# Five state-space products laid whole into the prompt attention, four attention output products into the sample attention

## What is computed

```python
glu = zg * sigmoid(zg @ w_glu + b_glu)              # branch A, the state-space model, 512 wide
a_br = glu @ w_ssm_out                              # 576 x 512 by 512 x 1024
b_br = o_nsa @ w_nsa_out                            # branch B, sparse attention, 576 x 512 by 512 x 1024
merged = sigmoid(g_a) * a_br + sigmoid(g_b) * b_br
x = x + merged @ w_o
```

## Time and profile before

| | |
|---|---|
| median of 3 runs | 796.8 us (795.71 to 800.57) |
| span of the profiled execution | 795.5 us |
| PE, matmuls | 762.2 us busy, 96% |
| PE, weight loads | 494.9 us busy, 62% |
| DVE | 379.9 us busy, 48% |
| ACT | 204.9 us busy, 26% |
| POOL | 106.8 us busy, 13% |
| the chain that ended last | PE 80%, DMA 8%, DVE 6%, issue 2%, ACT 2%, POOL 1% |
| prompt attention | 294 to 405 us |
| sample attention | 405 to 450 us |
| products and merge | 450 to 486 us |

### The profile page before, as it was taken

The page is one execution under the profiler, slowest core; times in us unless marked ns, Lnnn a source line. Parts: engine busy times, 40 slices in busy tenths (PEclk is TensorE's granted clock), DMA queues, the critical chain, the costliest instruction groups (busy, mean ns, idle before and its releaser), DMA issues.

```text
span 795.5 us, 12983 instructions
## 1 busy us (share of the span) xinstructions
PE 762.2 (96%) x5070; PEld 494.9 (62%) x5070; DVE 379.9 (48%) x850; ACT 204.9 (26%) x485; POOL 106.8 (13%) x160
## 2 busy tenths in 40 slices
PE   8999999999999999889999999999999999998995
PEld 5455588777778788555566775445556564654442
DVE  3269523997232323766624378434732212214865
ACT  3011213112223354654523200134111111123223
POOL 3000006000000311334500100011111101015002
PEclk9999999999999999999999999999999999999998
DMA  9640493841440499200030279003799999996002
GB/s 324 160 126 0 112 278 139 99 133 57 140 97 17 139 233 266 94 1 1 1 120 2 96 216 384 1 14 128 282 407 409 416 418 416 417 373 211 17 14 106
DMA packets 81287, 136.50 MB, mean 172 GB/s; under 512 B 33926, under 2 KB 57546, under 8 KB 77010
## 3 DMA queue, kind: packets, MB, share of 16 engines
q1 hardware_dynamic: 64700, 110.17, 41.7%
q0 software_dynamic: 3728, 13.38, 4.9%
q10 hardware_dynamic: 12798, 12.12, 4.6%
HBM read 116.55 MB, written 21.19 MB: 173 GB/s over the span
## 4 chain that ended last, share of the span: by engine, by line
PE 80%; DMA 8%; DVE 6%; issue 2%; ACT 2%; POOL 1%; DVEq 0%; SPq 0%; POOLq 0%; ACTq 0%
PE ps L1215 29%; PE ps L1300 10%; PE ps L1656 6%; PE ps L1904 5%; PE ps L1788 4%; PE ps L1222 3%; PE ps L1776 3%; DMA merged<-in_w_exp_down 3%; DMA w_slot<-in_w_exp_down 2%; PE ps L1441 2%; PE ps L1820 2%; PE ps L1491 2%; PE ps L1537 2%; PE ps L1518 2%; DMA wgu<-expert_rows,pos_i 1%
## 5 line engine op out<-in xcount | busy, mean ns | idle before, releaser
L1215 PE MATMUL ps<-w_slot,hT 128*128 128x396 f32 (+1 forms) x192 | 71.1, 529 | 0.6 <-DMA w_slot<-in_w_in 0.4
L1215 PE MATMUL ps<-hT,w_slot 128*128 128x288 f32 x256 | 63.1, 407 | 0.0
L1215 PEld LDWEIGHTS ps<-hT,w_slot 128*128 128x128 f32 x256 | 48.3, 190 | 13.9 <-issue 0.8
L1215 PEld LDWEIGHTS ps<-w_slot,hT 128*128 128x128 f32 x192 | 36.1, 190 | 32.5 <-issue 13.4
L2987 DVE SCALAR_TENSOR_TENSOR th<-th,ps 128x256 f32<-128x256 f32 x12 | 5.1, 421 | 103.2 <-ACT th L2248 103.2
L1788 PE MATMUL ps<-w_slot,hT 128*32 128x256 f32 x544 | 49.7, 380 | 0.0
L1300 PE MATMUL ps<-hT,w_slot 128*128 128x288 f32 x144 | 37.3, 407 | 0.0
L1215 PE MATMUL ps<-qg,w_slot 128*128 128x288 f32 x128 | 33.7, 408 | 0.0
L1788 PEld LDWEIGHTS ps<-w_slot,hT 128*32 128x32 f32 x544 | 26.3, 110 | 10.0 <-issue 2.3
L2728 DVE TENSOR_REDUCE nm_p<-ps 128x2 f32<-128x256 f32 (+3 forms) x32 | 25.0, 819 | 15.6 <-PE ps L1491 15.5
L1300 PEld LDWEIGHTS ps<-hT,w_slot 128*128 128x128 f32 x144 | 27.3, 190 | 7.6 <-issue 0.2
(11 more groups left out here) (508 smaller groups left out, 1416.5 us busy)
## 6 DMA issues: line engine op xcount, KB each, us to landing
merged<-in_w_exp_down SPq DMA_DIRECT2D x10, 1024.0 KB, 15.9
w_slot<-in_w_in SPq DMA_DIRECT2D x8, 1024.0 KB, 7.7
wgu<-in_w_exp_gate SPq DMA_DIRECT2D x8, 1024.0 KB, 12.1
wgu<-in_w_exp_up SPq DMA_DIRECT2D x8, 1024.0 KB, 14.1
w_slot<-in_w_exp_gate SPq DMA_DIRECT2D x8, 1024.0 KB
w_slot<-in_w_exp_up SPq DMA_DIRECT2D x8, 1024.0 KB
w_slot<-in_w_exp_down SPq DMA_DIRECT2D x6, 1024.0 KB
expert_rows<-onsaT ACTq DMA_DIRECT2D x12, 512.0 KB, 8.2
```

Of the source, the lines that this page charges most:

```text
L1215: ins = pe.matmul(out, a, b, start=(n == 0), stop=(n == len(pairs) - 1))
```

## The change

Five of the sixteen state-space products (m, h) = (0, 0), (0, 1), (1, 0), (1, 1), (2, 0) leave the sample attention and are laid at five places of the prompt attention. Each is whole: eight matmuls of the trace in one piece, into bank 6 or 7, which are free between two blocks there. ACT copies each out at a place of the list chosen for it (`ab_out` steps), and the values of the next block wait for that copy. In the sample attention, the eleven that are left take the first eleven iterations, and the four attention output products (0, 0), (1, 0), (2, 0), (3, 0) the last four: they use prompt rows only. DVE takes these four in the place of ACT, multiplies by the gate, and writes the result over the gate. The merge behind then has two operations for these four halves instead of three. Twelve `bb` products are left for the tail. `ab_out` lies in other tiles (a new one for m = 0 and 1, the end of `kvct` for 2, the queries for 3, keys and values for 4 to 7). Pairs of semaphores with separate times are joined into one, and one tile is allocated later in the list; neither changes an order.

```diff
-    steps, late, jobs = [], [], list(range(len(AB_JOBS)))
+    steps, late = [], []
+    jobs = [("ab", j) for j in range(AB_EARLY, len(AB_JOBS))] + [("bb", j) for j in range(len(BB_EARLY))]
...
-        steps.append(("ab", jobs.pop(0)))
-    return steps + [("ab", j) for j in jobs]
+        steps.append(jobs.pop(0))
+    return steps + jobs
...
+AB_BEFORE = {("vcs", 0, 0): [("ab", 0, 0), ("ab", 0, 1)], ("t", 2, 0): [("ab_out", 0, 0)],
...
+AB_BANK = [6, 7, 6, 6, 7]
+AB_OF_BLOCK = [1, 2, 4, 5]
...
-PROMPT = prompt_steps()
+PROMPT = [new for step in prompt_steps() for new in AB_BEFORE.get(step, []) + [step]]
...
+                elif what == "ab":
+                    if i == 0 and c == 0:
+                        pe.wait_ge(glu_made, 8)
+                        pe.wait_ge(*w_need["so"])
+                        pe.wait_ge(cmp_taken, COMPRESSED["kc", 0])
+                    elif i == 1 and c == 0:
+                        pe.wait_ge(cmp_taken, COMPRESSED["vcs", 0])
+                    elif i == 2 and c == 0:
+                        pe.wait_ge(pr_taken, 1)
+                    elif i == 3 and c == 0:
+                        pe.wait_ge(ab_taken, 3)
+                    elif i == 4 and c == 0:
+                        pe.wait_ge(pr_taken, 2)
+                    m, h = AB_JOBS[i]
+                    for j in (2 * c, 2 * c + 1):
+                        ins = pe.matmul(ps[:, AB_BANK[i], 0:HALF], wk("so", D, 0, 4)[:, j, P * m:P * m + P],
+                                        gluT[:, j, HALF * h:HALF * h + HALF], start=(j == 0), stop=(j == 3))
+                    if c:
+                        ins.then_inc(ab_made, 1)
...
+                    if first:
+                        pe.wait_ge(ab_taken, AB_OF_BLOCK[b])
...
+                elif what == "ab_out":
+                    m, h = AB_JOBS[i]
+                    act.wait_ge(ab_made, i + 1)
+                    act.activation(ab_out[m][:, HALF * h:HALF * h + HALF], ps[:, AB_BANK[i], 0:HALF], ACT.Copy).then_inc(ab_taken, 1)
...
+                elif what == "bb":
+                    m, h = BB_EARLY[i]
+                    dve.wait_ge(tg_ld[m], 16)
+                    v = gates[:, m, 1, HALF * h:HALF * h + HALF]
+                    o = take(("bb", m, h))
+                    empty(dve.scalar_tensor_tensor(v, v, 1.0, o[:, 0:HALF], ALU.add, ALU.mult))
+
+            dve.wait_ge(pe_done, PLAN.done(("o", len(GROUPS) - 1)))
+            dve.wait_ge(ab_taken, AB_EARLY)
```

More of the change, by code:

```diff
@@ L129 @@
 AB_JOBS = [(m, h) for m in range(KD) for h in range(2)]
+AB_EARLY = 5
+BB_EARLY = [(m, 0) for m in range(4)]
 def attention_steps():
-    steps, late, jobs = [], [], list(range(len(AB_JOBS)))
+    steps, late = [], []
+    jobs = [("ab", j) for j in range(AB_EARLY, len(AB_JOBS))] + [("bb", j) for j in range(len(BB_EARLY))]
     n = len(ITEMS)
@@ L376, in make_plan @@
             p.add(("ab",) + AB_JOBS[i], "act")
+        elif what == "bb":
+            p.add(("bb",) + BB_EARLY[i], "dve")
     for m in range(KD):
         for h in range(2):
-            p.add(("bb", m, h), "dve")
+            if (m, h) not in BB_EARLY:
+                p.add(("bb", m, h), "dve")
     for what, t, c in second_norm_steps():
@@ L516, in build @@
             onsaT = sb("onsaT", [P, 4, ROWS], stack=late)
-            ab_out = [(flat(qT) if m < 4 else flat(kv))[:, ROWS * (m % 4):ROWS * (m % 4 + 1)] for m in range(KD)]
             with ExitStack() as at:
@@ L1546, in _, with merge_product @@
             pe.wait_ge(qs_made, 1)
+            def merge_product(m, h):
+                cut = slice(HALF * h, HALF * h + HALF)
+                o = begin(("bb", m, h))
+                finish(product(o[:, 0:HALF], [(wk("no", D, 0, 4)[:, j, P * m:P * m + P], onsaT[:, j, cut]) for j in range(4)]))
             for what, i in attention_steps():
+                if what == "bb":
+                    pe.wait_ge(*w_need["no"])
+                    merge_product(*BB_EARLY[i])
+                    continue
                 if what == "ab":
@@ L1614, in _ @@
             pe.wait_ge(*emptied(("o", len(GROUPS) - 1)))
-            pe.wait_ge(*w_need["no"])
             for m in range(KD):
                 for h in range(2):
-                    cut = slice(HALF * h, HALF * h + HALF)
-                    o = begin(("bb", m, h))
-                    finish(product(o[:, 0:HALF], [(wk("no", D, 0, 4)[:, j, P * m:P * m + P], onsaT[:, j, cut]) for j in range(4)]))
+                    if (m, h) not in BB_EARLY:
+                        merge_product(m, h)
             def last_rows_through_w_o():
@@ L2026, in _ @@
             act.activation(sm[:, 9], sm[:, 6], ACT.Sin)
-            act.activation(sm[:, 10], sm[:, 7], ACT.Sin).then_inc(trig, 1)
+            act.activation(sm[:, 10], sm[:, 7], ACT.Sin).then_inc(dt_trig, 1)
             for t in range(NT - 1):
@@ L2798, in _ @@
                     cut = slice(HALF * h, HALF * h + HALF)
-                    dve.wait_ge(*emptied(("ab", m, h)))
+                    if AB_JOBS.index((m, h)) >= AB_EARLY:
+                        dve.wait_ge(*emptied(("ab", m, h)))
                     link(dve.scalar_tensor_tensor(mt[:, 0], gates[:, m % 4, 0, cut], 1.0, ab_out[m][:, cut], ALU.add, ALU.mult))
-                    o = take(("bb", m, h))
-                    empty(dve.scalar_tensor_tensor(mt[:, 1], gates[:, m % 4, 1, cut], 1.0, o[:, 0:HALF], ALU.add, ALU.mult))
+                    if (m, h) in BB_EARLY:
+                        second = gates[:, m, 1, cut]
+                    else:
+                        o = take(("bb", m, h))
+                        second = mt[:, 1]
+                        empty(dve.scalar_tensor_tensor(second, gates[:, m % 4, 1, cut], 1.0, o[:, 0:HALF], ALU.add, ALU.mult))
                     dve.wait_ge(*emptied(("bb", m, h)))
-                    tt(merged[:, m, cut], mt[:, 0], mt[:, 1], ALU.add).then_inc(merged_made, 1)
+                    tt(merged[:, m, cut], mt[:, 0], second, ALU.add).then_inc(merged_made, 1)
                     dve.wait_ge(merged_made, 2 * m + h + 1)
```

28 lines of the change are left out of this document (15 added, 13 removed), and 4 rows, old and new, of the table AB_BEFORE.

## The result

The changed kernel takes **790.1 us** (median of 5 runs, 789.1 to 792.0), the kernel before 796.8 us (794.9 to 800.6, 5 runs). The ratio is 0.991, with a 95% interval of 0.988 to 0.994. The forecast was 790.9 us within 1% of before, and both hold. The profiled execution has a span of 788.2 us, against 795.5.

The account below looks back on a forecast made before the run. TensorE (PE), busy 96% of the span, was taken as the bound. Tail -9.70 plus prompt attention +3.86 gave -5.84 us: profiled 789.7, median 1.3 above the span, so 790.9 us, range 787.5 to 795.0.

Parts of the forecast that it names:

- tail and loop: Sample attention loop keeps its length with 15 products; the tail goes from 18 products to 13, giving 9.70 us.
- first place: Prompt attention, before the compressed sample values: the product partly fills PE's 1.29 us wait for DVE's copy, +0.65 us.
- second place: Prompt attention, before the transposes of unit 4: no idle time to fill, so the full +2.04 us.
- third place: Prompt attention, before the compressed turn of unit 6: the product fills 0.85 us idle for DVE's copy, +1.11 us.
- fourth and fifth: Prompt attention, two products around the compressed scores of block 2, laid into PE's waits there: +1.04 us for both.
- ACT's copy at the fifth: ACT takes the fifth product behind unit 11's first exponentials, ahead of a turned copy, so the bank frees late: +0.45 us.
- clock: Prompt attention at 361 to 362 us: granted clock, 0.50 before, expected to stay high with pauses filled, -1.43 us.
- prompt part: Net cost of five early products in the prompt attention: 5.29 - 1.43 = 3.86 us, bounds nothing to 10.2.
- That more would be hidden: Rival: prompt attention has room for all 10.2 us by weight-load busy time, 785.7 us; chance 0.15.
- That the low clock stays: Rival: the low clock stays in the prompt attention or shows at another pause, 792.3 us; chance 0.17.
- No bank held PE: Rival: PE stands at banks awaiting ACT's copies at the five prompt attention places, +9 us, 800; chance 0.06.
- no gate came late: Rival: in the merge, the first of four gate tiles takes 7 us instead of 4, 792.9 us; chance 0.08.

Follow-up runs that it names:

- the first experiment: Changed kernel with all sixteen attention output products back in the tail, none in the last four sample attention steps; 796.3 us.
- the two experiments with these pauses, filled and open: Filled: kernel before plus idle transposes in two pauses of block 2, 797.3 us. Open: changed kernel without its fourth and fifth early products, 795.1 us.
- without fourth and fifth: Changed kernel without the two early products around the compressed scores of block 2, two attention output products more in the tail; 795.1 us.
- prompt part alone: Changed kernel with the five early state-space products kept and the four attention output products back in the tail; 796.3 us.
- gates behind `w_o`: Changed kernel with the load of `wo1` put ahead of the last four gate tiles, so these land later; 796.3 us.
- the kernel with the clock alone: Kernel before with unused transposes, seven ahead of block 2's compressed scores and twelve ahead of unit 11's masks, no product moved; 797.3 us.

## Why the prediction was right, step by step

The same numbers as the prediction's, now from rows of the changed kernel; a cost is the change in the distance between two starts. This is PE's timeline of the changed kernel at the first place, the third, and around the compressed scores of block 2, against the earlier trace rows:

```profile
319.04 0.43 PE L1469 MATMUL ps<-hT,cx 128*32 128x128 f32 x8 [0.30 <-ACT cx L2200]
319.40 2.21 PE L1500 MATMUL ps<-qg,w_slot 128*128 128x288 f32 x8
...
343.38 1.09 PE L1555 MATMUL ps<-ident,hT 128*128 128x128 f32 x8
344.31 2.11 PE L1500 MATMUL ps<-qg,w_slot 128*128 128x288 f32 x8
346.25 0.27 PE L1550 MATMUL ps<-ident,pc 128*128 128x128 f32 x1
346.36 0.60 PE L1540 MATMUL ps<-ident,caches 128*128 128x128 f32 x4
...
357.08 1.09 PE L1555 MATMUL ps<-ident,work 128*128 128x128 f32 x8
358.01 2.11 PE L1500 MATMUL ps<-qg,w_slot 128*128 128x288 f32 x8
359.95 1.00 PE L1511 MATMUL ps<-kcbd,qg 128*128 128x64 f32 x8
360.79 2.16 PE L1500 MATMUL ps<-qg,w_slot 128*128 128x288 f32 x8
362.78 0.39 PE L1522 MATMUL ps<-causal,ident_b 128*128 128x128 bf16 x4
363.10 1.56 PE L1528 MATMUL ps<-kt,qg 64*128 64x384 f32 x8
...
366.63 1.39 PE L1555 MATMUL ps<-ident,hT 128*128 128x128 f32 x8
```

| step | predicted | measured | from |
|---|---|---|---|
| tail and loop | -9.70 | -9.70 | marks |
| first place | +0.65 | +0.78 | 319.04 to 321.54, was 1.72 |
| second place | +2.04 | +2.04 | rows above |
| third place | +1.11 | +0.68 | 343.38 to 346.36, was 340.91 to 343.21 (the cached keys' turns) |
| fourth and fifth | +1.04 | +0.74 | 357.08 to 363.10, was 353.98 to 359.26 |
| ACT's copy at the fifth | +0.45 | +0.29 | eight transposes, 366.63 to 367.94, less 1.02 of pitch |
| clock | -1.43 | -1.58 | 363.10 to 368.96 (next masks) less 0.29, was 359.26 to 366.41 |
| prompt part | +3.86 | +2.93 | marks |

- **The tail was exact.** 104 matmuls in 25.22 us, and the fifteen steps of the sample attention kept their length with attention output products in four of them. That those four were not free to leave out is what the first experiment shows: they stand in pauses that PE would have otherwise.
- **The prompt part was charged 0.93 us too much**, the one part of the sum with errors of size. The mis-sized term is the pitch. I had taken 2.04 us for a product and 1.02 for eight turns, from rows in other surroundings. At the third and fourth places a product takes 1.94 (344.31 to 346.25, 358.01 to 359.95) and the turns ahead of it 0.93. The fifth takes 1.99 (360.79 to 362.78), the second the full 2.04, and the first, ahead of the narrow compressed values, 2.14 (319.40 to 321.54). What sets the pitch I did not work out. At the third place a short pause ahead of the cached keys' turns is filled as well: from the turn before to these 0.35 us in the kernel before, 0.11 now. The third, fourth and fifth places and ACT's copy together give 0.89 back, the clock 0.15, and the first place takes 0.13.
- **The clock came back as forecast.** The scores of unit 11 take 1.56 us again, and the two experiments with these pauses, filled and open, show each direction, each in one traced execution. The extra 0.15 us lies in the values behind the turns, which ran at the low level too (1.17 us from 363.20 to the next start, 1.02 at full clock) and which I had left out.
- **The merge kept up.** The new wait of DVE stands where it was forecast, 2.73 us long instead of 3.6. SP reached the gates earlier than I had taken it to, 10.9 us behind the start of the tail (463.79 less 452.85) and not 11.9, and the first tile landed 4.2 us later. DVE's timeline:

```profile
468.06 0.46 DVE L2856 SCALAR_TENSOR_TENSOR mt<-hT,kv 128x288 f32<-128x288 f32 x1 [2.73 <-DMA hT<-gates_by_features]
...
479.33 0.46 DVE L2407 TENSOR_TENSOR merged<-mt 128x288 f32<-128x288 f32 x1
```

and the row of PE that needs all sixteen halves:

```profile
481.60 7.09 PE L1240 MATMUL ps<-w_slot,merged 128*64 128x512 f32 x32
```

  The last half is ready at 479.79, so the cover is 1.8 us where I had worked out 1.0. Moving the loads in both directions shows that it is real: less wait brings nothing, and 4.9 us more of it exposes 3.15, which gives a cover of 4.87 - 3.15 = 1.7 us.
- **The rivals.** That more would be hidden is out: the second place paid in full. That the low clock stays is out for this stretch. No bank held PE, and no gate came late. So the sum was the forecast's, and the 0.8 us between 790.9 and 790.1 is of the size of the over-charged terms; with a scatter of some microseconds between executions, I don't claim more. Two of the prediction's sums were off, and neither bears on the forecast: 796.8 - 5.84 is 791.0 and not 790.9, and with 3 us more at each of the five places the banks would have cost 15 us, +9 on the kernel before, which is 806 us and not 800.
- **Where the margin was thin.** Three parts lost more when undone than the pauses that this opens: 7.05 us where they are 3.61 (four products), 5.3 where 4.4 was expected (fourth and fifth), 5.8 where 3.15 is exposed (gates). The forecast survived since the change opens no new pause of PE, not since I had understood what an open one costs; to that extent it was luck.

## What to carry to other kernels

Find room for matmul work by the idle time in PE's timeline at the very place, not by a busy share of a stretch: of five equal products, four cost 0.5 to 0.8 us each and one its full 2.04. When a stage's work is moved about, count a pause of PE that is opened or closed with what the granted clock does behind it, and read the windows for a few microseconds after it. A wait that is hidden today has a cover that can be worked out from two rows; write it down, since the next change will spend it.

## What the runs showed of the hardware that I had not expected

In the four places of the table a pause of PE, or several close together, costs its own length and then 0.6 to 1.2 times that again, for the clock goes to its low level behind it and stays there for some microseconds while PE is busy. The price is the stretch's time less the same instructions' time at full clock:

| kernel | idle on PE | ended at | low clock after | its price |
|---|---|---|---|---|
| before | 0.99, 0.51, 1.08 with short work between | 359 us | to past 363 us | 1.6 us |
| without fourth and fifth | 0.72, 0.51, 1.09 | 362.4 | past 368 us | 2.7 us |
| prompt part alone | 0.94, 0.97, 1.08, 0.62 | 451.9 | to about 458 us | 3.1 us |
| gates behind `w_o` | 3.15 in one | 484.4 | to about 490 us | 2.9 us |

In the second kernel the scores of unit 11 start at 362.76 and the next masks at 371.05, 8.29 us, against 5.57 for the same in the kernel with the clock alone (359.45 to 365.02). The changed kernel still has 5.00 us of pauses in its prompt attention, one of 1.14 us among them, and its granted clock is 1.00 throughout. The pause in the last stage, shown above, is no rule either: behind 2.02 us of it the clock stayed at 1.00 in the kernel before, and behind 2.06 us it fell in the kernel with the clock alone. So the length of a pause doesn't settle it, and what else does I can't say from these runs. The Trainium skill describes the direction (TensorE: Matmul & The Clock Gate, Part 1, What's actually happening): "the default state is throttled, and activity releases the throttle"; the rows agree, and the price is theirs.

The granted clock goes with the larger part of the scatter between executions of one kernel. Over the 32 compared executions of the kernel before in the two groups its mean goes from 0.987 to 0.997, and the span falls with it (correlation -0.87): 800.0 us at 0.987, 792.6 at 0.997. At one value, 0.995, spans from 794.9 to 797.3 us are left. One low period at a place where another execution has none, as in the last stage of the kernel with the clock alone, is worth 1.7 us there. That is why the marks in one stage say more here than the difference of two spans.
